# A two-block fp32 transformer kernel: where transposes, the last FFN product's token blocks and early weight loads stand

## The chip, the cores and the metric

The kernel runs on one core of a Trainium2 chip. The metric is the device time of one execution in microseconds (us), as a median of several runs. The core has five engines that run their own instruction lists and meet at semaphores: TensorE (PE, matmuls; its weight loads are listed as PEld), VectorE (DVE), ScalarE (ACT), GpSimd (POOL), and SyncE (SP), which here only issues DMAs. TensorE works with one of two clocks, 1.2 and 2.4 GHz; the profile gives the granted clock as a share of the full one.

## The reference

Two blocks, one after the other, on 1024 tokens of width 1024, all in fp32:

```python
def first_block(x, ...):
    proj = rms_norm(x, norm_mix) @ w_in
    aq, ak, av, rq, rk, rv, rg, ga, gr = jnp.split(proj, offsets, axis=-1)
    att = sliding_window_attention(aq, ak, av, att_sinks)      # 8 heads, 2 key/value heads
    ret = head_group_norm(retention_chunkwise(rq, rk, rv), ret_gn_gain) * jax.nn.silu(rg)
    merged = jax.nn.sigmoid(ga) * (att @ w_att_o) + jax.nn.sigmoid(gr) * (ret @ w_ret_o)
    x = x + merged @ w_out
    h = rms_norm(x, norm_ffn)
    x = x + (jax.nn.silu(h @ w_gate) * (h @ w_up)) @ w_down    # D_FF 2816
    return rms_norm(x, final_norm)

def second_block(x, ...):
    q, k, v, zu, zv = jnp.split(rms_norm_2(x, g_pre_mix) @ w_in, [512, 1024, 1536, 2048], axis=-1)
    sgu = spatial_gating(jax.nn.gelu(zu), jax.nn.gelu(zv), sgu_ln_g, sgu_ln_b, sgu_w, sgu_b)
    mix = jnp.concatenate([dilated_attention(q, k, v, rel_bias), sgu], axis=-1) @ w_out
    x = x + rms_norm_2(mix, g_post_mix)
    f = jnp.square(jax.nn.relu(rms_norm_2(x, g_pre_ffn) @ w_ff1)) @ w_ff2      # width 4096
    return x + rms_norm_2(f, g_post_ffn)
```

## The kernel before

**Products.** Each fp32 operand is split into a high part (type fp32r) and a low part (the rest), and a product is three matmuls: high by low, low by high, high by high. Activations stand in HH and HL (high, low), weights in WH and WL. A matmul has 128 rows of one operand and 512 columns of the other. A weight "unit" is 128x1024, loaded raw by SP into one of three slots of WRAW (`fetch`, L2505; a slot is reused once both halves of its former weights are split), rounded into WH by ACT (L1014, in FFN down products L1222) and subtracted into WL by DVE (L1476, L1762) or POOL (L2162).

**Order.** Nothing schedules the program: each engine has a Python function (`pe_program`, `act_program`, `dve_program`, `pool_program`, `sync_program`) that writes out its instructions in the order in which they run, and all of them walk the same lists of keys. `Banks` (L66) gives the eight PSUM banks to results in turn, in PE's order, so an engine may fill a bank only when what was in it before has been read.

**First projections.** After the attention projections PE runs the loop over `RVG`, groups of 24 matmuls that make the retention values: group (nh, tt) is `proj_n` (L636 to L638), 128 tokens by 512 columns. Ahead of groups 0 and 1, `values(0)` and `values(1)` (L685, matmuls of L689) transpose the tile AVT, which DVE copies out of the two banks of the projection `av` (L1546); that projection stands directly before the loop (L620 to L622). `put` moves results of both kinds from PSUM through two buffers FA, and SP stores them; `FILLS` (L347) is the list of what goes through FA, in order. From group 1 on `turn0` (L692) adds transposes of X tiles.

**FFNs.** In both blocks the up and down products follow Strassen and Winograd with seven products P1 to P7 of half-size quarters. `strassen(lay)` makes the hidden activations; they go to DRAM (`scr_h`, from the tile HS) and come back as quarters A11, A21, A12, A22 of the down product's operand (`load_quarter`, L2745, into HHF and HLF). Each quarter is loaded in two halves, here called A11/0 and A11/1. At the last block of the up product SP issues them at set steps (`FIRST_IN`): A11/0 and A21/0 when P1 has ended, A12/0 and A22/0 at P5, A11/1 and A21/1 at P2, A12/1 and A22/1 at P4. Between them it issues the first raw weights of the down product, two items in each: d0 (items 0 and 1), d1 (items 2 and 3), d2, d3 and so on. `ffn_down` (PE: L851) then runs, for each product and each chunk of the inner dimension, the items of a chunk (5 or 6 in layer 1, 8 in layer 2) by four token blocks of 128: three matmuls each (L864 to L866). An item needs its weights' two halves and its operand's two halves, DAH and DAL, which ACT and DVE make (L1219, L1759) in a ring of eight. In all products but the last PE takes an item for all four token blocks and then the next item. In the last product, P4, it takes token block by token block, all items each (L876), as the rows of a block are then complete and what follows can begin.

**Behind the down product.** DVE adds a block's product to the residual rows X (L1850, instruction L1882), after POOL has added the sum DV into X (L2351). In layer 1 the norm of the second block follows: row norms, HLF by L1935, and `back(3, tt)` (PE: L643, transposes of L650; ACT: L1027, L1031; DVE: L1484, L1489) turns the normed tokens of tile tt into HH and HL. Tiles 0 to 3 are turned between the blocks of P4, and tiles 4 to 7 in the loop over `zv` (PE L892, ACT L1332), one behind each group of 24 matmuls. Ahead of that loop PE runs the four `zu` products (L620), which need `back(3, 0)` to `back(3, 3)`. In layer 2 the last instructions are the final norm's: `fin` on DVE (L2130, L2144) with POOL's reciprocal roots (L2205) and the stores.

## Time and profile before

| what | value |
|---|---|
| median of 3 runs | 2671.52 us (2671.32 to 2673.26) |
| the profiled execution | 2674.15 us |
| its span, first to last instruction | 2672.4 us |
| mean granted TensorE clock | 0.996 |
| PE busy | 2627.6 us (98% of the span) |
| DVE, POOL, ACT busy | 1550.4, 1174.9, 1026.5 us |
| chain that ended last: PE, DVE, POOL, DMA, issue | 88%, 4%, 3%, 2%, 2% |
| largest waits of PE | L650 for DVE X 9.1 us in 2, L864 for DVE WL 5.6 us in 7, L811 for DVE HS 3.1 us, L689 for DVE AVT 2.3 us |

Times of the trace are counted from the start of the span; 1.75 us of the profiled execution lie around the span. A row of the timeline gives the start, the duration, engine, line, operation, tiles, a count, and in brackets how long the engine was idle before it and what released it. Matmuls overlap: one lasts 0.39 us, and the next starts 0.23 us after it where nothing is late, so the time lost at a wait is read from start to start.

### The profile page before, as it was taken

The numbers are of one execution on the slowest core, as the hardware profiler recorded it, in microseconds if no ns is written. First come the engines' busy times: TensorE is split into PE (matmuls) and PEld (weight loads), VectorE is DVE, ScalarE is ACT, GpSimd is POOL, SyncE is SP. The second block draws the span as 40 slices with busy tenths as digits, with TensorE's granted clock in tenths as the row PEclk, the third lists the DMA queues.
The fourth block names the chain that finished last, engine by engine and source line by source line (L and its number), as shares of the span: only waits on it lengthen the run. The fifth ranks groups of instructions, "written<-read, shape, count | busy, mean of one in ns | idle before, by whom it ended". The sixth has DMA issues, their size and how long they took to land.

```text
span 2672.4 us, 35524 instructions
## 1 busy us (share of the span) xinstructions
PE 2627.6 (98%) x13170; PEld 2203.9 (82%) x13170; DVE 1550.4 (58%) x2631; ACT 1026.5 (38%) x2053; POOL 1174.9 (44%) x933
## 2 busy tenths in 40 slices
PE   8999999999999999999999999999999999999998
PEld 7788888777888988888888778989988888878886
DVE  4325555575535544444798641167647666568787
ACT  4122333574223332322444631067634332244443
POOL 1347877344535566555232764244144544200204
PEclk9999999999999999999999999999999999999999
DMA  5555766704551222222752344233043333263524
GB/s 182 177 181 201 268 230 235 268 17 151 197 195 64 72 87 87 79 80 71 283 187 94 118 154 159 74 69 65 20 142 103 107 114 107 103 251 131 189 96 164
DMA packets 162618, 372.35 MB, mean 139 GB/s; under 512 B 21478, under 2 KB 42598, under 8 KB 158822
## 3 DMA queue, kind: packets, MB, share of 16 engines
q1 hardware_dynamic: 162446, 370.08, 40.4%
q8 instruction: 106, 1.74, 0.3%
q14 instruction: 66, 0.53, 0.1%
HBM read 267.94 MB, written 101.83 MB: 138 GB/s over the span
## 4 chain that ended last, share of the span: by engine, by line
PE 88%; DVE 4%; POOL 3%; DMA 2%; issue 2%; ACT 1%; SPq 0%; POOLq 0%; DVEq 0%; ACTq 0%
PE PS L811 12%; PE PS L813 12%; PE PS L814 12%; PE PS L864 5%; PE PS L866 5%; PE PS L865 5%; PE PS L636 4%; PE PS L638 4%; PE PS L637 4%; PE PS L965 3%; PE PS L620 3%; PE PS L621 3%; PE PS L622 3%; PE PS L749 1%; PE PS L943 1%
## 5 line engine op out<-in xcount | busy, mean ns | idle before, releaser
L2162 POOL TENSOR_TENSOR WL<-WRAW,WH 128x512 fp32r<-128x512 f32 (+1 forms) x146 | 246.7, 1690 | 363.6 <-ACT WH L1014 363.6
L811 PE MATMUL PS<-HH,WL 128*128 128x512 f32 (+1 forms) x928 | 349.3, 376 | 5.3 <-DVE HS L1804 3.1
L814 PE MATMUL PS<-HH,WH 128*128 128x512 f32 (+1 forms) x928 | 347.8, 375 | 0.0
L813 PE MATMUL PS<-HL,WH 128*128 128x512 f32 (+1 forms) x928 | 347.6, 375 | 0.0
L1476 DVE TENSOR_TENSOR WL<-TS,WH 128x512 fp32r<-128x512 f32 x216 | 227.2, 1060 | 182.0 <-ACT WH L1014 181.7
L864 PE MATMUL PS<-WH,DAL 128*128 128x512 f32 x756 | 295.8, 391 | 5.6 <-DVE WL L1762 5.6
L866 PE MATMUL PS<-WH,DAH 128*128 128x512 f32 x756 | 294.7, 390 | 0.0
L865 PE MATMUL PS<-WL,DAH 128*128 128x512 f32 x756 | 294.7, 390 | 0.0
L2351 POOL TENSOR_TENSOR X<-X,DV 128x512 f32<-128x512 f32 x56 | 90.1, 1632 | 358.2 <-DVE DV L1874 275.5
L1014 ACT ACTIVATE WH<-TS 128x512 fp32r<-128x512 f32 x216 | 130.9, 623 | 199.2 <-POOL TS L2178 199.1
L811 PEld LDWEIGHTS PS<-HH,WL 128*128 128x128 f32 x928 | 174.8, 188 | 37.2 <-DVE HS L1804 3.3
L636 PE MATMUL PS<-WH,HL 128*128 128x512 f32 x512 | 203.9, 398 | 1.2 <-DVE HL L2041 0.9
L638 PE MATMUL PS<-WH,HH 128*128 128x512 f32 x512 | 200.7, 392 | 0.0
L814 PEld LDWEIGHTS PS<-HH,WH 128*128 128x128 f32 x928 | 174.8, 188 | 31.2
L637 PE MATMUL PS<-WL,HH 128*128 128x512 f32 x512 | 200.5, 392 | 0.0
L813 PEld LDWEIGHTS PS<-HL,WH 128*128 128x128 f32 x928 | 174.8, 188 | 31.0
L1014 ACT ACTIVATE WH<-WRAW 128x512 fp32r<-128x512 f32 (+1 forms) x236 | 175.4, 756 | 61.3 <-PE PS L638 18.7
L2178 POOL TENSOR_TENSOR TS<-WRAW 128x512 f32<-128x512 f32 x108 | 143.8, 1331 | 124.4 <-issue 120.8
L1476 DVE TENSOR_TENSOR WL<-WRAW,WH 128x512 fp32r<-128x512 f32 (+1 forms) x90 | 115.1, 1280 | 105.1 <-ACT WH L1014 105.0
L864 PEld LDWEIGHTS PS<-WH,DAL 128*128 128x128 f32 x756 | 142.3, 188 | 37.7 <-issue 6.0
L1762 DVE TENSOR_TENSOR WL<-WRAW,WH 128x512 fp32r<-128x512 f32 x189 | 155.8, 824 | 24.1 <-ACT WH L1222 23.9
L866 PEld LDWEIGHTS PS<-WH,DAH 128*128 128x128 f32 x756 | 142.3, 188 | 29.9
(372 smaller groups left out, 6142.1 us busy)
## 6 DMA issues: line engine op xcount, KB each, us to landing
WRAW<-in_u_f SPq DMA_DIRECT2D x56, 512.0 KB, 3.6
WRAW<-in_u_in SPq DMA_DIRECT2D x54, 512.0 KB, 4.5
WRAW<-scr_t SPq DMA_DIRECT2D x52, 512.0 KB, 3.7
scr_h<-HS SPq DMA_DIRECT2D x96, 256.0 KB, 2.2
WRAW<-in_u_gu SPq DMA_DIRECT2D x44, 512.0 KB, 3.4
scr_t<-TTa SPq DMA_DIRECT2D x19, 1024.0 KB, 4.1
WRAW<-in_u_out SPq DMA_DIRECT2D x24, 512.0 KB, 3.5
scr_x<-X SPq DMA_DIRECT2D x24, 512.0 KB, 5.0
```

What stands on the lines that cost most here:

```text
L636: e.matmul(PS[:, b, :], HL[:, k, ts], whole_slot(WH, n)[:, cs], start=(k == 0), stop=False)
L637: e.matmul(PS[:, b, :], HH[:, k, ts], whole_slot(WL, n)[:, cs], start=False, stop=False)
L638: mm = e.matmul(PS[:, b, :], HH[:, k, ts], whole_slot(WH, n)[:, cs], start=False, stop=(k == 7))
L811: e.matmul(PS[:, b, 0:wd], wl[:, blk(kk)], op_moving(q, kk, c0, wd, 0), start=(kk == 0), stop=False)
L813: e.matmul(PS[:, b, 0:wd], wh[:, blk(kk)], op_moving(q, kk, c0, wd, 1), start=False, stop=False)
L814: mm = e.matmul(PS[:, b, 0:wd], wh[:, blk(kk)], op_moving(q, kk, c0, wd, 0), start=False, stop=(kk == 3))
L864: e.matmul(dst, hl, wh, start=(i == 0), stop=False)
L865: e.matmul(dst, hh, wl, start=False, stop=False)
L866: mm = e.matmul(dst, hh, wh, start=False, stop=(i == g - 1))
L1014: e.activation(dst, src, ACT.Copy).then_inc(*c.inc("w_hi", i))
L1476: e.tensor_tensor(lo, raw, hi.bitcast(F32), ALU.subtract).then_inc(*c.inc("w_lo_v", i))
L2162: e.tensor_tensor(lo, raw, hi.bitcast(F32), ALU.subtract).then_inc(*c.inc("w_lo_p", i))
```

## The change

In the loop over `RVG`, group 0 now stands before `values(0)` and group 1 before `values(1)`, on PE, ACT and SP, and `FILLS` has the same order. In the last product of both down products, PE takes token blocks 0 and 1 together, item by item, and then blocks 2 and 3 alone; in layer 1 `back(3, 0)` and `back(3, 1)` stand behind the pair, `back(3, 2)` and `back(3, 3)` behind block 2, and none behind block 3. DVE follows with its own order. `back(3, 4 + tt)` moves one zv group later on PE and ACT. On SP, the raw weights d0 to d2 are fetched at P6 of the last block of the up product, and the rest of the first product's (d3, in layer 2 alone) at P2, each ahead of the quarter loads of that step. Before, d0 and d1 were fetched at P7, d2 at P2 behind its quarter loads, and d3 at P4 behind its quarter loads.

```diff
--- before.py
+++ after.py
@@ -344,8 +344,8 @@
     PAIRS_OF = {1: 0, 2: FF1 // 2}
     T_SLOT = {"T3": 0, "T4": 1, "T1": 2, "T2": 3}
     RVG = [("rv", nh, tt) for nh in range(2) for tt in range(NT)]
-    FILLS = ([("aq", j, half) for half in range(2) for j in range(4)] + [("ak", 0), ("ak", 1), ("avt", 0), RVG[0],
-             ("avt", 1)] + RVG[1:])
+    FILLS = ([("aq", j, half) for half in range(2) for j in range(4)] + [("ak", 0), ("ak", 1), RVG[0], ("avt", 0), RVG[1],
+             ("avt", 1)] + RVG[2:])
     EARLY = [("ak", 0), ("ak", 1), ("av", 0)]
     IN_ORDER = [(p, 0, m, 0) for m in range(NB0) for p in ("P1", "P6", "P7", "P5", "P2", "P4", "P3")]
     LATE = [("zu", j, 1) for j in range(4)] + [("q2", j, half) for j in range(8) for half in range(2)]
@@ -697,9 +697,9 @@
             mm.then_inc(*bk.fill(("nb", 1, q, j)))
 
         for i, (_, nh, tt) in enumerate(RVG):
+            proj_n(("rv", nh, tt), [U["u_rv", 4 * nh + x] for x in range(4)], tt, tt == 0)
             if i < 2:
                 values(i)
-            proj_n(("rv", nh, tt), [U["u_rv", 4 * nh + x] for x in range(4)], tt, tt == 0)
             if 1 <= i <= len(TURN0):
                 turn0(*TURN0[i - 1])
         for j in range(4):
@@ -874,11 +874,13 @@
                         for b in range(4):
                             part(i, b)
                 else:
-                    for b in range(4):
+                    for bs in ((0, 1), (2,), (3,)):
                         for i in range(g):
-                            part(i, b)
-                        if lay == 1:
-                            back(3, b)
+                            for b in bs:
+                                part(i, b)
+                        if lay == 1 and bs[0] < 3:
+                            back(3, bs[0])
+                            back(3, bs[0] + 1)
                 for i in range(g):
                     used(DOP[lay, n, i], d_key(lay, n, 3))
             LAST[ops[DOP[lay, last - 1, g - 1]][2] + 1] = d_key(lay, last - 1, 3)
@@ -892,8 +894,8 @@
         for tt in range(NT):
             normed(3, [tt])
             proj_n(("zv", tt), [U["u_zv", i] for i in range(4)], tt, tt == 0)
-            if tt < 4:
-                back(3, 4 + tt)
+            if 1 <= tt < 5:
+                back(3, 3 + tt)
             for i in buckets_after(tt):
                 b = open_bank(("bp", i))
                 w.wait_ge(*c.at("buckets", "all"))
@@ -1078,9 +1080,9 @@
         for half in range(2):
             feed(("av", half))
         for i, key in enumerate(RVG):
+            put(key)
             if i < 2:
                 put(("avt", i))
-            put(key)
             if 1 <= i <= len(TURN0):
                 turn0(*TURN0[i - 1])
             if i < 15:
@@ -1334,8 +1336,9 @@
             w.wait_ge(*bk.full(key))
             e.activation(V2[:, tt, :], PS[:, bk.at(key), :], ACT.Gelu_apprx_tanh).then_inc(*bk.free(key))
             feed(key)
+            if 1 <= tt < 5:
+                back(3, 3 + tt)
             if tt < 4:
-                back(3, 4 + tt)
                 scale_x2(4 + tt)
         for j in range(4):
             zu(j, 1)
@@ -1907,9 +1910,10 @@
             for b in range(4):
                 add(last - 2, b)
             for b in range(4):
-                if lay == 1:
-                    back(3, b)
                 add(last - 1, b)
+                if lay == 1 and b in (1, 2):
+                    back(3, 2 * b - 2)
+                    back(3, 2 * b - 1)
                 if lay == 2:
                     fin(1, b)
             feed(d_key(lay, last - 2, 3))
@@ -2590,9 +2594,9 @@
             feed(("av", half))
             down_tiles(("av", half))
         for i, key in enumerate(RVG):
+            put(key)
             if i < 2:
                 put(("avt", i))
-            put(key)
             if i < 15:
                 feed(key)
             down_tiles(key)
@@ -2762,15 +2766,13 @@
                 for x, (p, q) in enumerate(PROD):
                     key = p, lay, m, c0
                     if (m, c0, wd) == BLOCKS[lay][-1]:
+                        while p == "P6" and n_fetch[0] <= DUNIT[lay, 0, 4]:
+                            fetch()
+                        while p == "P2" and n_fetch[0] < DUNIT[lay, 1, 0]:
+                            fetch()
                         for kind, half in FIRST_IN.get(p, ()):
                             w.wait_ge(*bk.full(key))
                             load_quarter(lay, 0, kind, half)
-                        while p == "P7" and n_fetch[0] <= DUNIT[lay, 0, 2]:
-                            fetch()
-                        while p == "P2" and n_fetch[0] <= DUNIT[lay, 0, 4]:
-                            fetch()
-                        while p == "P4" and n_fetch[0] < DUNIT[lay, 1, 0]:
-                            fetch()
                     if (lay == 2 or m % 2 == 1) and p in DONE:
                         qq = DONE[p]
                         if lay == 1:
```

SP, last block of the up product of layer 2. HHF and HLF are the quarters' tiles, `WRAW<-in_u_f` raw weights (d0 to d3 in turn), `scr_h<-HS` a store of hidden activations; in brackets are the semaphores waited for. Before:

```order
L2530 DMA WRAW<-in_u_f 128x2x512 [waits w_lo_v]
L2530 DMA WRAW<-in_u_f 128x2x512 [waits w_t,w_lo_p]
L2757 DMA HHF<-scr_h 128x4x512 [waits bank_full7]
L2757 DMA HLF<-scr_h 128x4x512
L2781 DMA scr_h<-HS 128x512 [waits f_m2]
L2757 DMA HHF<-scr_h 128x4x512 [waits h11_0,h22_0,h12_0,h21_0,bank_full0]
L2757 DMA HLF<-scr_h 128x4x512
L2530 DMA WRAW<-in_u_f 128x2x512 [waits w_lo_v]
L2781 DMA scr_h<-HS 128x512 [waits f_s]
L2757 DMA HHF<-scr_h 128x4x512 [waits bank_full1]
L2757 DMA HLF<-scr_h 128x4x512
L2530 DMA WRAW<-in_u_f 128x2x512 [waits w_lo_v]
```

and after the change:

```order
L2534 DMA WRAW<-in_u_f 128x2x512 [waits w_lo_v]
L2534 DMA WRAW<-in_u_f 128x2x512 [waits w_t,w_lo_p]
L2534 DMA WRAW<-in_u_f 128x2x512 [waits w_lo_v]
L2761 DMA HHF<-scr_h 128x4x512 [waits bank_full7]
L2761 DMA HLF<-scr_h 128x4x512
L2783 DMA scr_h<-HS 128x512 [waits f_m2]
L2534 DMA WRAW<-in_u_f 128x2x512 [waits w_lo_v]
L2761 DMA HHF<-scr_h 128x4x512 [waits h11_0,h22_0,h12_0,h21_0,bank_full0]
L2761 DMA HLF<-scr_h 128x4x512
L2783 DMA scr_h<-HS 128x512 [waits f_s]
L2761 DMA HHF<-scr_h 128x4x512 [waits bank_full1]
L2761 DMA HLF<-scr_h 128x4x512
```

d2, the third load of WRAW, moved from behind A11/1 and A21/1 (waits on h11_0 and bank_full0) up to d0 and d1, and d3, the fourth, from the last place to just ahead of A11/1. It waits for a low half made by DVE, and the quarters now stand behind that wait. In layer 1 the same holds for d2; d3 belongs there to the second product and keeps its place.

DVE, the end of the down product of layer 1: L1882 adds a block of P4 to X, L1489 makes HL for half a token tile in `back`. Before:

```order
L1878 TENSOR_TENSOR DV<-PS,DV 128x512 [waits bank_free5,bank_full5]
L1489 TENSOR_TENSOR HL<-PS,HH 128x4x128 [waits h_hi] x2
L1882 TENSOR_TENSOR X<-PS,X 128x512 [waits d_v,bank_full6]
L1489 TENSOR_TENSOR HL<-PS,HH 128x4x128 [waits h_hi] x2
L1882 TENSOR_TENSOR X<-PS,X 128x512 [waits d_v,bank_full1]
L1489 TENSOR_TENSOR HL<-PS,HH 128x4x128 [waits h_hi] x2
L1882 TENSOR_TENSOR X<-PS,X 128x512 [waits d_v,bank_full4]
L1489 TENSOR_TENSOR HL<-PS,HH 128x4x128 [waits h_hi] x2
L1882 TENSOR_TENSOR X<-PS,X 128x512 [waits d_v,bank_full7]
L1476 TENSOR_TENSOR WL<-WRAW,WH 128x1024 [waits w_hi] x3
```

and after, where the same lines are numbered 1885, 1492 and 1479:

```order
L1881 TENSOR_TENSOR DV<-PS,DV 128x512 [waits bank_free5,bank_full5]
L1885 TENSOR_TENSOR X<-PS,X 128x512 [waits d_v,bank_full6]
L1885 TENSOR_TENSOR X<-PS,X 128x512 [waits d_v,bank_full7]
L1492 TENSOR_TENSOR HL<-PS,HH 128x4x128 [waits h_hi] x4
L1885 TENSOR_TENSOR X<-PS,X 128x512 [waits d_v,bank_full4]
L1492 TENSOR_TENSOR HL<-PS,HH 128x4x128 [waits h_hi] x4
L1885 TENSOR_TENSOR X<-PS,X 128x512 [waits d_v,bank_full1]
L1479 TENSOR_TENSOR WL<-WRAW,WH 128x1024 [waits w_hi] x3
```

The add of block 1 moved ahead of all of `back(3, 0)` and `back(3, 1)`, and the last add stands behind `back(3, 3)` as the last of the group. POOL's instructions have the same order before and after.

## Rows read from the trace of the kernel before

**Rows 1.** Page, part 1: busy time, share of the span and instructions of each engine.

```profile
PE 2627.6 (98%) x13170; PEld 2203.9 (82%) x13170; DVE 1550.4 (58%) x2631; ACT 1026.5 (38%) x2053; POOL 1174.9 (44%) x933
```

**Rows 2.** Timeline, PE, values: start us, us, line, operation, count, [idle before <-releaser].

```profile
89.52 0.39 PE L622 MATMUL PS<-HH,WH 128*128 128x512 f32 x1
...
92.24 0.87 PE L689 MATMUL PS<-ID,AVT 128*128 128x128 f32 x4 [2.34 <-DVE AVT L1546]
...
99.80 0.60 PE L689 MATMUL PS<-ID,AVT 128*128 128x128 f32 x4
...
105.73 0.49 PE L696 MATMUL PS<-ID,X 128*128 128x128 f32 x3
```

**Rows 3.** Timeline, DVE: low half of the first u_rv unit, copies into AVT.

```profile
66.40 1.23 DVE L1476 TENSOR_TENSOR WL<-WRAW,WH 128x1024 fp32r<-128x1024 f32 x1 [4.50 <-ACT WH L1014]
...
91.41 1.28 DVE L1546 COPY AVT<-PS 128x512 f32<-128x512 f32 x2
```

**Rows 4.** Windows: us, busy (x) of PE, PEld, DVE, ACT, POOL, granted clock, DMA share, GB/s.

```profile
92.00:96.00 4.00, 3.76 (x12) 3.11 (x13) 0.69 (x2) 0.60 (x1) 1.71 (x1) 0.57 0.32 58
...
2345.00:2355.00 10.00, 10.00 (x46) 8.29 (x45) 7.01 (x12) 4.42 (x8) 0.00 (x0) 1.00 1.04 390
...
2376.00:2379.00 3.00, 2.78 (x7) 2.24 (x8) 3.00 (x6) 3.00 (x7) 0.00 (x0) 0.50 0.29 107
```

**Rows 5.** Timeline, PE, start of the second down product of layer 1.

```profile
1299.20 0.47 PE L864 MATMUL PS<-WH,DAL 128*128 128x512 f32 x1 [0.16 <-DVE WL L1762]
...
1305.43 0.47 PE L864 MATMUL PS<-WH,DAL 128*128 128x512 f32 x1 [0.51 <-DVE WL L1762]
```

**Rows 6.** Chain of waits, pieces in order of time, start of the down product, layer 1.

```profile
1279.39 8.76 DMA WRAW<-in_u_dn
```

**Rows 7.** Timeline, PE, layer 2: items 6 and 8 of the down product.

```profile
2367.88 0.47 PE L864 MATMUL PS<-WH,DAL 128*128 128x512 f32 x1 [0.57 <-DVE WL L1762]
...
2376.22 0.77 PE L864 MATMUL PS<-WH,DAL 128*128 128x512 f32 x1 [2.62 <-DVE WL L1762]
```

**Rows 8.** Chain of waits, same place: start us, us, piece.

```profile
2353.18 13.11 DMA WRAW<-in_u_f
...
2370.73 3.96 DMA WRAW<-in_u_f
```

**Rows 9.** Timeline, DVE, same place.

```profile
2346.67 0.68 DVE L1762 TENSOR_TENSOR WL<-WRAW,WH 128x512 fp32r<-128x512 f32 x1
...
2368.86 0.68 DVE L1826 TENSOR_TENSOR HS<-PS,HS 128x512 f32<-128x512 f32 x1
```

**Rows 10.** Operations on tile HHF, 2345 to 2348: durations ns, starts, issue to landing.

```profile
L2757 SPq DMA_DIRECT2D HHF<-scr_h x1: 359/359/359, 2345.9 to 2345.9; - x1
...
DMA to landing us min/median/max: 8.0/8.0/8.0
```

**Rows 11.** Timeline, PE, end of FFN 1 and zv loop.

```profile
1500.59 0.47 PE L620 MATMUL PS<-HH,WL 128*128 128x512 f32 x1 [1.80 <-DVE HL L1489]
...
1529.15 1.09 PE L650 MATMUL PS<-ID,HLF 128*128 128x128 f32 x8 [1.08 <-DVE HLF L1935]
```

**Rows 12.** Timeline, DVE, end of FFN 1.

```profile
1495.54 0.69 DVE L1882 TENSOR_TENSOR X<-PS,X 128x512 f32<-128x512 f32 x1 [0.59 <-POOL X L2351]
...
1501.10 4.95 DVE L1476 TENSOR_TENSOR WL<-WRAW,WH 128x1024 fp32r<-128x1024 f32 x2
```

**Rows 13.** Timeline, POOL, end of FFN 1.

```profile
1491.67 9.96 POOL L2351 TENSOR_TENSOR X<-X,DV 128x512 f32<-128x512 f32 x8
```

**Rows 14.** Timeline, PE, last product of FFN 2.

```profile
2644.47 0.47 PE L864 MATMUL PS<-WH,DAL 128*128 128x512 f32 x1 [1.26 <-DVE WL L1762]
...
2645.67 0.47 PE L864 MATMUL PS<-WH,DAL 128*128 128x512 f32 x1 [0.28 <-DVE WL L1762]
```

**Rows 15.** Timeline, POOL and DVE, last product of FFN 2.

```profile
2646.20 12.01 POOL L2351 TENSOR_TENSOR X<-X,DV 128x512 f32<-128x512 f32 x8 [5.08 <-DVE DV L1878]
...
2662.99 0.69 DVE L1882 TENSOR_TENSOR X<-PS,X 128x512 f32<-128x512 f32 x1 [1.59 <-PE PS L866]
```

## The prediction

> **What bounds the kernel now.** The page's busy times come first: PE is busy for 2627.6 us, 98% of the span [rows 1], so PE is the bound, and what a change of order can give lies in the 45 us in which PE waits. These I read next, one wait of PE at a time: in the timeline the bracket names the releaser, and the loss is the distance from start to start less the 0.23 us of a matmul that nothing holds up. Then comes the granted clock: where it is 0.5 the matmuls go at 1.2 GHz instead of 2.4, and a wait costs more than itself. Last, behind each wait, the engine that it names, to find what that engine waited for.
>
> The change touches five places where PE waits.
>
> **A, values.** The last matmul of the projection starts at 89.52, the transposes of AVT at 92.24 [rows 2]: they wait for DVE's copies, which run from 91.41 to 92.7 [rows 3]. The loss is 2.72 - 0.23 = 2.49 us. Behind it four transposes and 24 matmuls take 7.56 us (92.24 to 99.80), while the next such group takes 5.93 (99.80 to 105.73) [rows 2]; in between the granted clock is 0.57 [rows 4], so 1.63 us are lost to the lower clock. Now 24 matmuls that need no copy stand first. Their weights' first unit was split at 66.40 [rows 3], some 23 us ahead; their banks are bank 0 and on, which other results left long before. So group rv0 runs from 89.75 to 95.3, and AVT has been there since 92.7. Both losses go: **-4.1 us**. The bank that DVE's copy frees is now asked for by the transposes, 3 us after it is free. ACT's `put` of rv0 now stands ahead of the AVT results: nobody waits for those within 10 us.
>
> **B1, raw weights of FFN 1.** PE waits at 1299.20 and 1305.43 for WL, 0.16 and 0.51 us [rows 5]; each gap adds some 0.16 us until matmuls overlap again, so 0.32 + 0.67. Why: d2 was issued at 1279.39 behind quarter loads and took 8.76 us to land [rows 6]; DVE's splits of its items stand ahead of the P3 add, that add ahead of POOL's product, the store and the fetch of d3 on SP. Fetched at P6, d2 is in by about 1278. Then the chain is ended by A11/1, which now has d2's 0.5 MB ahead of it (1.3 us at the 390 GB/s that such a stretch moves [rows 4]): it lands near 1285.5, the P3 add comes 2.6 us sooner, and so do d3 and d4. 2.6 is more than 0.51: **-1.0 us**.
>
> **B2, raw weights of FFN 2.** Item 6 starts at 2367.88 [0.57] and item 8, the first of the second product, at 2376.22 [2.62] [rows 7]. d3 was issued at 2353.18 and took 13.11 us, since three quarter halves were ahead of it on a queue at 390 GB/s; it landed at 2366.3 [rows 4, 8]. DVE splits items 4 to 7 before the P3 add (2368.86 [rows 9]); the store of that block follows, and only then d4, issued at 2370.73, 3.96 us [rows 8], landing at 2374.7. Back from item 6 without its wait (2367.15), at 12 matmuls or 2.73 us an item, item 4 is due at 2361.7 and item 8 at 2372.6. The losses are 0.73 at item 6, 2.62 + 0.16 at item 8 and, from 2376 to 2379 at clock 0.50 [rows 4], half of some 3.2 us, 1.6. After: d2 goes out with d0 and d1 and lands near 2346.3. d3 waits for the low half of item 1, which DVE starts at 2346.67 [rows 9], is issued near 2347.5 and lands near 2354. A11/1, which had landed at 2345.9 + 8.0 = 2353.9 [rows 10], has 1 MB more ahead of it, 2.7 us at 390 GB/s: near 2356.6, 5 us before item 4 is due. The P3 add is then paced by A11/1 and four splits of some 1.2 us, near 2362. d4 follows 1.9 us later as before (2368.86 to 2370.73), lands near 2368, and ACT and DVE need the 1.5 us that they need now (2374.7 to 2376.22): 2369.5 against 2372.6. All three losses go: **-5.1 us**.
>
> A rule of the Trainium skill bears on this, in DMA: Bandwidth & Descriptors, section "Queues, rings and completion order": descriptors of a ring are taken in the order in which they were queued. By it an early d3 has to push A11/1 back by its full size, and that is the 2.7 us worked out above from the 390 GB/s. The trace agrees, as the late d3 took 13.11 us behind the quarters [rows 8].
>
> **C1, end of FFN 1.** The first zu matmul starts at 1500.59 [1.80] [rows 11]. It waits for HL of `back(3, 3)`, which is behind the adds on DVE. These go at the pace of POOL, whose eight adds of 1.25 us run from 1491.67 to 1501.6 [rows 13]; block 1's add starts at 1495.54 [rows 12]. Moving the transposes earlier doesn't change POOL. After: adds 0 and 1 on DVE (until 1496.15), `back(3, 0)` and `back(3, 1)`, four HL of 0.6, add 2, four more HL: 1496.15 + 2.4 + 0.6 + 2.4 = 1501.6, where before the last HL was done just ahead of 1500.59. (L1882 and L1489 handle tiles of one shape, 0.6 us apart.) The banks say the same of PE: `back(3, 3)` takes the bank that the add of block 1 frees at 1496.15, so PE stands for about 2 us before block 3 instead of 1.8 us before zu, and zu starts at 1501.9. That is **+1.3 us**: the wait moves and grows. **C1b**: in the zv loop PE waits at 1529.15 for HLF [1.08] [rows 11], 1.24 us with the gap; one group (5.5 us) later HLF is there. **-1.2 us**. The next `back` has a small wait of the same kind, taken as nothing.
>
> What comes behind C1: DVE's two splits of units start at 1501.10 and take 4.95 us together [rows 12], where one alone takes 1.23 [rows 3]; POOL works beside them. They now start a little later. The Trainium skill, SBUF — State Buffer, section "SBUF: two separate sides", says that a DVE operation with two inputs in SBUF and a GpSimd operation lock each other out for the whole instruction, so that the one that comes second waits for the other. By it the first split would go from behind POOL's split instead of ahead of it, and be ready up to 3 us later; the 4.95 us agree. By my rows, the second zu product starts 5.4 us after the first, near 1507.3, and splits that end at 1506 to 1507.5 just make it. I take 0 and keep 1 us for the range.
>
> **C2, end of FFN 2.** PE waits at 2644.47 [1.26] and 2645.67 [0.28] [rows 14]: the last product's block 0 needs an item each 0.68 us, and DVE, between other work, makes the low half of the last item just ahead of 2645.67. With two blocks per item it needs one each 1.36 us; the 1.26 + 0.28 and two gaps, 1.86 us, go, and PE ends 1.9 us sooner. Behind PE stand DVE's add of the last block at 2662.99 and 9.4 us of norm and store up to the end. POOL's adds into X take until 2658.2 [rows 15] and don't move, but the last block's add comes only at 2661. Between 1.4 and 1.9, as the norm of block 2 comes closer to POOL's: **-1.4 us**.
>
> **The sum**: -4.1 - 1.0 - 5.1 + 1.3 - 1.2 - 1.4 = -11.5 us. The profiled execution took 2674.15 us and would take 2662.6; the median of the runs is 2.6 below it, and the same sum against 2671.52 gives 2660.0. That is my forecast.
>
> **The rivals.**
> - *The wait just moves, and the clock goes with it.* The new 2 us of PE before block 3 at 1494 could be followed by a stretch at half clock, as after the 2.34 us of A and the 2.62 us of B2; that of 1.80 at 1500.59 was not. Price 1.6, and 1 us more if the second zu product comes late: 2661.6 to 2662.6. For it: 2.0 lies between 1.80 and 2.34.
> - *B gives little.* If the early raw weights only push the quarters back, and the P3 add stays where it is, B2's 5.1 stays: 2665.1. Against it: item 4 has 5 us to spare.
> - *C2 gives nothing.* If blocks 0 and 1, handed over together, make DVE and POOL the last ones at the end: 2661.4. For it: POOL is busy until 2658.2 [rows 15].
> - *The change doesn't do what it says at A*: rv0 waits for weights or a bank. Then 4.1 less: 2664.1. Against it: 66.40 [rows 3].
> - *Slower than before.* On SP, d3's fetch waits for a low half with A11/1, A21/1, A12/1 and A22/1 queued behind it. If DVE reaches that half later than at 2346.67 by more than 5 us, item 4 waits, and with it everything. A delay of w then costs w - 5 at item 4, and B2's 5.1 isn't gained, which leaves 6.4 of the gain: even at w = 11.4, and slower by 0.2% (5.3 us) from w = 16.7, at 2676.9. Nothing on DVE holds that half back so long: what is ahead of it are splits of 0.68.
>
> **How the numbers follow.** Forecast, all terms within their bounds, 2657.5 to 2662.5: 0.57. The moved wait with the clock: 0.14. B gives little, or half: 0.09. C2 nothing: 0.05. A nothing: 0.04. Two of these together, or something that I don't see, near no change: 0.07. Slower: 0.04. A measurement of this kernel can tell about 0.2%, 5.3 us, from no change, so faster means below 2666.2. The first five cases lie below it, the sixth within 0.2% (B and A nothing: 2669.2). Faster 0.57 + 0.14 + 0.09 + 0.05 + 0.04 = 0.89, same 0.07, slower 0.04. The range reaches from 2656, where the bounds of C1 (0 instead of +1.3), C2 (-1.9) and small waits (-0.9) add up, to 2665.5, which takes in B giving little.
>
> **What would show it.** In the profile after: no wait before L689 near 95 and clock 1.00 from 92 to 96; turn0's first transposes near 101.6; no wait above 0.3 us at items 6 and 8 of FFN 2 and no stretch at 0.5 near 2364 to 2370; d3 landing before 2356; a wait of PE of about 2 us inside P4 of layer 1, and nearly none before zu; HLF's wait in the zv loop gone; PE's last matmul about 12 us earlier. Wrong it would be with A11/1 landing after item 4 is due, or with a half-clock stretch at a place that had none.

## The result and the profile after

Over 20 runs of each kernel in turns, the changed kernel took 2671.03 us in the median (2658.05 to 2676.21) and the kernel before 2675.39 (2671.10 to 2689.16); the ratio on record is 0.9961, with a 95% interval of 0.9944 to 0.9978, so 10.4 us faster (6 to 15). The ratio of the two medians alone would be 0.9984, 4.4 us. These numbers can't be read without knowing that the executions of both kernels fall into two groups, a short one at a mean granted clock of 0.995 to 0.998 and a long one at 0.990 to 0.993, and that the medians depend on how many fell into which. Over all runs of this study the kernel before has 60 short executions (median 2672.4) and 57 long ones (2686.4), with one of 3300 us at a clock of 0.749 left out; the changed kernel has 9 short (2659.4) and 11 long (2674.0). Group against group it is 13.1 and 12.4 us faster. My forecast was 11.5, given as 2660.0 against a median of before that came from short executions alone; the profiled execution of after is a short one too, 2659.72 us, with a span of 2657.9 instead of 2672.4. What the long group is, is told behind the experiments.

Page of the changed kernel, busy times and the chain that ended last:

```profile
PE 2622.1 (99%) x13170; PEld 2202.3 (83%) x13170; DVE 1550.7 (58%) x2631; ACT 1027.2 (39%) x2053; POOL 1177.2 (44%) x933
...
PE 90%; DVE 4%; POOL 3%; issue 1%; DMA 1%; ACT 1%; POOLq 0%; DVEq 0%; SPq 0%; ACTq 0%
```

PE has 5.5 us less of busy time for the same matmuls, some 3.2 of them from the two stretches at half clock that are gone (A and B2), and 9 us less of waiting.

**Values.** Timeline of PE, the places of [rows 2], and windows of the granted clock (the second one covers the start of the second product of layer 2, for below):

```profile
89.62 0.39 PE L636 MATMUL PS<-WH,HL 128*128 128x512 f32 x1
...
95.07 0.60 PE L689 MATMUL PS<-ID,AVT 128*128 128x128 f32 x4
...
101.00 0.60 PE L689 MATMUL PS<-ID,AVT 128*128 128x128 f32 x4
...
101.44 0.60 PE L696 MATMUL PS<-ID,X 128*128 128x128 f32 x4
```

```profile
92.00:96.00 4.00, 4.00 (x22) 3.31 (x21) 0.06 (x1) 0.67 (x2) 1.36 (x1) 1.00 0.34 124
...
2366.00:2372.00 6.00, 6.00 (x28) 4.99 (x27) 6.00 (x11) 5.59 (x12) 0.00 (x0) 1.00 0.34 122
```

Group rv0 starts at 89.62, the transposes of AVT stand behind it and wait for nothing, and turn0 begins at 101.44 instead of 105.73. From the last matmul of the projection to there it is 12.04 us instead of 16.21.

**Start of the FFN 2 down product.** SP's queue and DVE's P3 add, for [rows 8 to 10]:

```profile
2339.90 0.37 SPq L2534 DMA_DIRECT2D WRAW<-in_u_f  x1
...
2340.83 0.36 SPq L2761 DMA_DIRECT2D HHF<-scr_h  x1
...
2355.58 8.17 SPq L2534 DMA_DIRECT2D WRAW<-in_u_f  x4
```

```profile
2353.71 0.68 DVE L1829 TENSOR_TENSOR HS<-PS,HS 128x512 f32<-128x512 f32 x1
```

d3 (2339.90) took 5.6 us to land instead of 13.11; A11/1 (2340.83) took 7.3. The product itself starts 7.54 us earlier than before, so on the scale of before d3 landed at 2353.0, A11/1 at 2355.7, the P3 add came at 2361.3 and d4 was issued at 2363.1. PE had no wait at items 6 and 8, and the clock stayed at 1.00. From the first matmul of L864 to the 61st PE took 46.04 us before and 40.80 now. In layer 1, where the whole product starts 4.20 us earlier, the P3 add came 5.47 us behind the first matmul instead of 8.15, 2.7 us sooner.

**End of FFN 1.** POOL, PE and DVE, for [rows 11 to 13]:

```profile
1482.14 2.38 POOL L2166 TENSOR_TENSOR WL<-WRAW,WH 128x1024 fp32r<-128x1024 f32 x1 [2.13 <-ACT WH L1016]
...
1484.48 10.00 POOL L2355 TENSOR_TENSOR X<-X,DV 128x512 f32<-128x512 f32 x8
```

```profile
1482.76 1.16 PE L650 MATMUL PS<-ID,HLF 128*128 128x128 f32 x8 [0.72 <-DVE DV L1881]
...
1489.19 1.16 PE L650 MATMUL PS<-ID,HLF 128*128 128x128 f32 x8 [0.76 <-DVE X L1885]
...
1494.68 0.47 PE L620 MATMUL PS<-HH,WL 128*128 128x512 f32 x1 [0.69 <-DVE HL L1492]
```

```profile
1488.36 0.69 DVE L1885 TENSOR_TENSOR X<-PS,X 128x512 f32<-128x512 f32 x1 [1.80 <-POOL X L2355]
...
1494.94 4.12 DVE L1479 TENSOR_TENSOR WL<-WRAW,WH 128x1024 fp32r<-128x1024 f32 x2
```

PE waits twice by some 0.7 us inside the product, and 0.69 us before zu, where it had one wait of 1.80 and three of 0.2 to 0.4. In the zv loop the transposes behind the second group start without a wait; before, this was the row at 1529.15:

```profile
1527.44 1.03 PE L650 MATMUL PS<-ID,HLF 128*128 128x128 f32 x8
```

**End of FFN 2.** PE's last matmul, POOL and DVE:

```profile
2647.72 0.39 PE L866 MATMUL PS<-WH,DAH 128*128 128x512 f32 x1
```

```profile
2637.19 8.27 POOL L2355 TENSOR_TENSOR X<-X,DV 128x512 f32<-128x512 f32 x5
```

```profile
2648.56 0.68 DVE L1885 TENSOR_TENSOR X<-PS,X 128x512 f32<-128x512 f32 x1
...
2653.55 1.28 DVE L2134 SCALAR_TENSOR_TENSOR X<-XG,SM,NXb 128x1024 f32<-128x1024 f32 x1 [0.44 <-POOL SM L2209]
```

The last add comes at 2648.56, the last product of the norm at 2653.55. Segment by segment, in us, from the starts of the same instructions in the two profiles:

| segment | forecast | measured |
|---|---|---|
| up to turn0 (A) | -4.1 | -4.3 |
| FFN 1, first 61 matmuls of L864 (B1) | -1.0 | -1.2 |
| from there to zu (C1) | +1.3 | -0.5 |
| zu to the second attention (C1b) | -1.2 | -1.8 |
| FFN 2, first 61 matmuls of L864 (B2) | -5.1 | -5.2 |
| from there to the end (C2) | -1.4 | -1.66 |
| all else | 0 | +0.3 |
| sum | -11.5 | -14.4 |

Five of the six terms are within 0.6 us of the forecast, and one has the wrong sign: C1.

### The profile page after: what moved, and what is told of

It is laid out like the page before. It is cut to its first block, busy times and chain, and to the rows that moved or that the text cites. A ratio compares the mean times of both kernels' runs of the same rounds, so it can differ in the third digit from the quotient of the medians.

```text
span 2657.9 us, 35523 instructions
## 1 busy us (share of the span) xinstructions
PE 2622.1 (99%) x13170; PEld 2202.3 (83%) x13170; DVE 1550.7 (58%) x2631; ACT 1027.2 (39%) x2053; POOL 1177.2 (44%) x933
## 4 chain that ended last, share of the span: by engine, by line
PE 90%; DVE 4%; POOL 3%; issue 1%; DMA 1%; ACT 1%; POOLq 0%; DVEq 0%; SPq 0%; ACTq 0%
PE PS L811 13%; PE PS L813 13%; PE PS L814 13%; PE PS L866 6%; PE PS L864 6%; PE PS L865 6%; PE PS L636 3%; PE PS L638 3%; PE PS L637 3%; PE PS L967 3%; PE PS L620 3%; PE PS L621 3%; PE PS L622 3%; PE PS L749 1%; PE PS L945 1%
## 5 line engine op out<-in xcount | busy, mean ns | idle before, releaser
L864 PE MATMUL PS<-WH,DAL 128*128 128x512 f32 x756 | 294.3, 389 | 0.0
L811 PEld LDWEIGHTS PS<-HH,WL 128*128 128x128 f32 x928 | 174.7, 188 | 37.2 <-DVE HS L1807 3.3
L865 PEld LDWEIGHTS PS<-WL,DAH 128*128 128x128 f32 x756 | 141.9, 188 | 29.6
L864 PEld LDWEIGHTS PS<-WH,DAL 128*128 128x128 f32 x756 | 141.9, 188 | 29.4 <-DVE DV L1881 0.2
```

Source lines behind the costliest of these rows:

```text
L811: e.matmul(PS[:, b, 0:wd], wl[:, blk(kk)], op_moving(q, kk, c0, wd, 0), start=(kk == 0), stop=False)
L864: e.matmul(dst, hl, wh, start=(i == 0), stop=False)
L865: e.matmul(dst, hh, wl, start=False, stop=False)
```

## The experiments

Each kernel was profiled once and timed. As the two groups blur medians of ten runs, I read each part in its segment of the profile, and the times group by group.

### Part A alone

The hunks on `FILLS` and on the three `RVG` loops, on the kernel before.

> The kernel before with part A alone: group rv0 ahead of values(0), rv1 ahead of values(1), nothing else. My theory: both the wait of PE before L689 (2.34 us) and the half-clock stretch behind it (1.63 us) go, so that turn0's first transposes start near 101.6 instead of 105.73, and all that follows is 4.1 us earlier; the waits further on are those of the kernel before. Rival (the clock falls somewhere else instead): the stretch at half clock turns up later and only 2.5 us are won.

```profile
94.04 0.60 PE L689 MATMUL PS<-ID,AVT 128*128 128x128 f32 x4
...
100.41 0.60 PE L696 MATMUL PS<-ID,X 128*128 128x128 f32 x4
```

turn0 begins at 100.41. PE reached the last matmul of the projection at 88.37, 1.15 us earlier than in the profile of before and ahead of every edit; from there it took 12.04 us, as in the changed kernel. The waits further on are in the same places, but not of the same size: in layer 2 the wait at item 6 (0.57 us before) is missing, as d3 took 11.79 us to land instead of 13.11, and the stretch to the 61st matmul took 44.91 us instead of 46.04. Seven short executions have a median of 2670.8, three long ones 2685.9, so 1.6 and 0.5 us less than before; the short ones alone spread over 7 us, so these times can't tell 2.5 from 4.1. The profiles of other kernels can: the stretch at half clock behind this wait isn't always there. In the profile of part C1 alone, which has the old order here, PE waits as before:

```profile
88.60 0.39 PE L622 MATMUL PS<-HH,WH 128*128 128x512 f32 x1
...
91.32 0.63 PE L689 MATMUL PS<-ID,AVT 128*128 128x128 f32 x4 [2.33 <-DVE AVT L1548]
...
97.26 0.60 PE L689 MATMUL PS<-ID,AVT 128*128 128x128 f32 x4
...
103.18 0.60 PE L696 MATMUL PS<-ID,X 128*128 128x128 f32 x4
```

```profile
91.00:95.00 4.00, 3.68 (x19) 3.14 (x20) 0.78 (x2) 0.60 (x1) 1.81 (x1) 1.00 0.30 56
```

The window has clock 1.00, and turn0 begins 14.58 us after the last projection matmul, against 16.21 in the profile of before. The 1.63 us of the clock are real in one execution and absent in another; of the six profiles with the old order at this place three have the stretch, the kernel before among them, and three do not. Against the 12.04 us of the new order, A is thus worth 2.5 us in three of these profiles and 4.1 to 4.2 in the other three.

### Part B alone, and one step of it

The SP hunk alone.

> The kernel before with the SP part alone: raw weights of the down products' first items fetched at P6 and P2 of the last block. My theory: 1.0 us in layer 1 (waits at 1299.20 and 1305.43 gone) and 5.1 us in layer 2 (waits of items 6 and 8 and the half-clock stretch gone), 6.1 in all. Rival: the quarters land later by as much as the weights land sooner, so item 4 of layer 2 waits and only 0 to 3 us are won.

From the first to the 61st L864 it took 40.80 us in both layers, as in the changed kernel: 1.2 and 5.2 us saved against the profile of before. Other profiles with the old order have 42.02 to 42.23 us in layer 1 and 44.91 to 45.99 in layer 2, so that B is worth 1.2 to 1.4 and 4.1 to 5.2 us. Short executions 2666.9 (3), long ones 2680.4 (7), so 5.5 and 6.0 us less. The rival is out: no item waited for its quarter.

Then one line only:

```diff
+                        while p == "P4" and n_fetch[0] < DUNIT[lay, 1, 0]:
+                            fetch()
                         for kind, half in FIRST_IN.get(p, ()):
                             w.wait_ge(*bk.full(key))
                             load_quarter(lay, 0, kind, half)
...
-                        while p == "P4" and n_fetch[0] < DUNIT[lay, 1, 0]:
-                            fetch()
```

> The kernel before with one line moved on SP: at P4 of the last block, the fetch of what is left of the first down product (d3, in layer 2) stands ahead of the loads of A12/1 and A22/1 instead of behind them; d0 to d2 stay. It asks how much of part B hangs on how early d3 is. By 1 MB at 390 GB/s d3 lands 2.7 us sooner, 2363.6 instead of 2366.3 on the scale of the kernel before; item 6's wait (0.57) goes, the P3 add and d4 come 2.7 us sooner, so the 2.62 us at item 8 become 0 to 0.3, and with them the half-clock stretch goes: 4.5 to 5.1 us in layer 2, nearly all of the SP part. Rival (the two steps that the changed kernel moves it are needed): at least 1.5 us of wait stay at item 8. Layer 1 has no d3 in this product and stays as it was.

DVE and SP in this kernel:

```profile
2362.39 0.68 DVE L1826 TENSOR_TENSOR HS<-PS,HS 128x512 f32<-128x512 f32 x1
...
2351.77 0.37 SPq L2530 DMA_DIRECT2D WRAW<-in_u_f  x1
...
2364.26 1.82 SPq L2530 DMA_DIRECT2D WRAW<-in_u_f  x3
```

d3 took 7.5 us to land, so at 2359.3. Counted from the product's first matmul it landed 6.6 us sooner than before and not 2.7: it was issued 1.0 us earlier, and the two half quarters that were ahead of it are 2 MB, not 1 as I had written. The P3 add came at 2362.39, d4 at 2364.26, and the segment took 40.80 us. The whole of the 5.2 us of layer 2 thus hangs on one place: d3 ahead of the last two quarter halves. Seven short executions: 2667.0, 5.4 less than before; three long ones: 2681.7. That d2 and d3 go even earlier in the changed kernel adds nothing in layer 2; what d2 adds is the 1.2 us of layer 1.

### Part C1 alone, and the changed kernel without it

PE's pair and DVE's order, for layer 1 only:

```diff
-                    for b in range(4):
+                    for bs in (((0, 1), (2,), (3,)) if lay == 1 else ((0,), (1,), (2,), (3,))):
```

> The kernel before with the pair of token blocks in the last product of layer 1 alone (PE, and DVE's order), back(3, 4 + tt) left in its place. Measured from the start of POOL's eight adds into X (1491.67 in the kernel before, zu at 8.92 us behind it), my theory has zu's first matmul at 10.2 us behind it, so 1.3 us later. Rival (the pair itself makes zu start sooner, as the changed kernel's zu started 0.7 us sooner than parts A and B explain): zu at 8.9 us or less behind the start of POOL's adds. If the start of POOL's adds moves, it is by the load of the first zu weights, which takes 5.53 us in the profile of before and 3.79 in that of after.

```profile
1487.58 10.02 POOL L2354 TENSOR_TENSOR X<-X,DV 128x512 f32<-128x512 f32 x8
```

```profile
1497.79 0.47 PE L620 MATMUL PS<-HH,WL 128*128 128x512 f32 x1 [0.63 <-DVE HL L1491]
```

zu came 10.21 us behind the start of POOL's adds, in the changed kernel 10.20, in kernels without the pair 8.9 (8.87 to 9.32 in seven). The +1.3 us of the forecast is right, as a distance from POOL's start. The short executions of this kernel took 2671.6 (8) and the long ones 2688.3 (2), against 2672.4 and 2686.4: no difference that these few can tell. What moved is the start of the adds. The chain of waits leads from it back through POOL's and ACT's halves of the first zu weights to their load, here in the changed kernel, then in the kernel before:

```profile
1477.19 3.79 DMA WRAW<-in_u_in
```

```profile
1482.61 5.53 DMA WRAW<-in_u_in
```

Without the pair this load took 5.53, 5.19, 5.3, 5.3, 5.5, 5.4 and once 4.5 us; with the pair 3.79, 3.53, 3.5, 3.6 and 3.4, but 4.6 and 5.4 in two more kernels. It is issued 158.0 us behind the 61st matmul in both profiles shown, so the place of the issue didn't move. SP issues two more of the same size within 0.9 us behind it; the one after those, issued alone, took 3.3 to 3.5 us in every kernel. So with the pair the first load is mostly faster by 1.7 us, but not always, and I have no row that says why. That stays open.

The other direction, PE and DVE of layer 1 as before, all else as changed:

> The changed kernel with one part undone: in the last product of layer 1 PE takes token block by token block again, with back(3, b) behind each, and DVE has its old order; back(3, 4 + tt) keeps its new place one zv group later. My theory: zu's first matmul 8.9 us behind the start of POOL's adds instead of 10.2; the load of the first zu weights, 5.2 to 5.5 us in the kernels without the pair and 3.5 to 3.8 with it so far, takes about 5.3 again, so that the two cancel and the time stays within 0.5 us; the wait of PE for HLF in the zv loop (0.7 to 1.3 us in all kernels with the old place) stays gone. Rival (the load's duration has nothing to do with the pair): 3.8 us, and 1.3 us faster than the changed kernel.

zu 8.9 us behind POOL's start, load 5.3 us, no wait in the zv loop, span 2657.4 (2657.9 with the pair), and the five short executions at 2659.9 against 2659.4 (the three long ones at 2676.3 against 2674.0). In these runs the pair in layer 1 gives nothing: in the distance from the 61st matmul to zu, the seven kernels without it have 175.3 to 176.0 us and the five with it, and POOL's split in its old place, 175.2 to 176.4. Where the load took about the same, the 1.3 us come out: 176.4 with the pair and a load of 4.64 us (the changed kernel with the wait filled, below), where PE stood for 1.60 us inside the product, and 175.3 without the pair and a load of 4.48 us (part B alone).

What does give something is the later `back` in the zv loop. With the old place PE waited there for HLF by 0.69 to 1.39 us, and in one profile by 3.65, with half clock behind it:

```profile
1529.63 1.09 PE L650 MATMUL PS<-ID,HLF 128*128 128x128 f32 x8 [3.65 <-DVE HLF L1938]
```

### Part C2 alone, and with two pairs

> The kernel before with the pair of token blocks in the last product of layer 2 alone. My theory: waits of 1.26 and 0.28 us near 2644 gone, PE's last matmul 1.9 us earlier, the end 1.4 to 1.9 us earlier. Rival: DVE and POOL become the last ones and the end moves by less than 0.5 us.

The waits near 2644 are gone, from the 61st matmul to PE's last it took 263.61 us instead of 265.69, and 10.21 us follow instead of 9.79: 1.66 us in all, the same as in the changed kernel. Short executions 2669.9 (6), 2.5 less; of the others three are long (2680.2 to 2686.7) and one lies between, 2674.6 at a clock of 0.994. The next kernel gives the last two blocks to PE as a pair too:

```diff
-                    for bs in ((0, 1), (2,), (3,)):
+                    for bs in (((0, 1), (2,), (3,)) if lay == 1 else ((0, 1), (2, 3))):
```

> The changed kernel, but in layer 2's last product blocks 2 and 3 are a pair as well. PE needs no more weights per time than it has, so its end stays. My theory: both last blocks come at PE's end, DVE and POOL have two norms behind it instead of one, and the kernel ends 2 to 3 us later. Rival (DVE and POOL are behind anyway): within 0.5 us.

DVE in this kernel, the adds of blocks 2 and 3 and the last product of the norm:

```profile
2662.47 0.69 DVE L1885 TENSOR_TENSOR X<-PS,X 128x512 f32<-128x512 f32 x1 [5.64 <-PE PS L866]
...
2665.69 0.68 DVE L1885 TENSOR_TENSOR X<-PS,X 128x512 f32<-128x512 f32 x1
...
2670.69 1.28 DVE L2134 SCALAR_TENSOR_TENSOR X<-XG,SM,NXb 128x1024 f32<-128x1024 f32 x1 [0.44 <-POOL SM L2209]
```

PE ends as in the changed kernel, but the add of block 2 waits until then (2662.47; PE's last matmul starts at 2662.73), that of block 3 stands 3.2 us behind it, and from PE's last matmul to the end it is 12.3 us instead of 10.2: 2.1 us slower. Short executions 2660.9 (4), long ones 2676.5 (6), 1.6 and 2.5 more than the changed kernel. A last block alone is worth that.

### What sets zu: a later split

If POOL's eight adds set when zu starts, then POOL's split ahead of them is what to move:

```diff
-                    feed(d_key(lay, last - 3, 3))
+                    if lay == 2:
+                        feed(d_key(lay, last - 3, 3))
                 for b in range(4):
                     add_v("21", "P7", b)
                     add_v("22", "P7", b)
+                    if lay == 1 and b == 1 and k == len(CHUNKS[lay]) - 1:
+                        feed(d_key(lay, last - 3, 3))
```

and on DVE `back(3, 2)` and `back(3, 3)` stand ahead of the add of block 2.

> The changed kernel with POOL's split of the first zu unit moved behind four of its eight adds into X at the end of layer 1, and on DVE the add of block 2 moved behind back(3, 2) and back(3, 3). Theory (POOL's adds, started late by a load, set when zu starts): the adds start some 1.9 us sooner, PE's wait for the bank of block 1's add (0.76 us) goes, and zu starts 1.3 to 1.7 us sooner, the kernel is as much faster. Rival (the load and the split themselves become the last ones): zu moves by less than 0.5 us.

POOL and PE:

```profile
1482.95 5.04 POOL L2358 TENSOR_TENSOR X<-X,DV 128x512 f32<-128x512 f32 x4 [2.68 <-DVE DV L1881]
...
1487.95 2.39 POOL L2169 TENSOR_TENSOR WL<-WRAW,WH 128x1024 fp32r<-128x1024 f32 x1
...
1490.28 5.07 POOL L2358 TENSOR_TENSOR X<-X,DV 128x512 f32<-128x512 f32 x4
```

```profile
1483.02 1.16 PE L650 MATMUL PS<-ID,HLF 128*128 128x128 f32 x8 [0.71 <-DVE DV L1881]
...
1492.83 0.39 PE L620 MATMUL PS<-HH,WL 128*128 128x512 f32 x1
...
1547.17 1.87 PE L902 MATMUL PS<-OH,RB 33*8 33x512 f32 x4 [0.88 <-DMA RB<-in_c_one]
```

From the 61st matmul to zu it took 173.41 us instead of 175.52, and PE went into zu without a wait: 2.1 us. POOL's adds started 163.5 us behind the 61st matmul instead of 165.3. Two orders changed at once here, POOL's and DVE's, and no run separates them. From zu to the second block's attention this profile then took 249.78 us instead of 246.64 and so gave the gain back: a wait of 0.41 us at the second zu product, and 55 us behind zu one of 0.88 us for the table of relative positions, whose load SP issued at 1543.11, 1.1 us later than in the changed kernel, with 3.4 us at half clock behind it. Two short executions at 2657.6, ten long at 2670.0: 1.7 and 4.0 us less than the changed kernel. The theory on POOL holds for the start of zu, and the next one in line was a load.

## The long executions

The profile of part B alone is a long one. PE and windows of it in the second block's attention:

```profile
1746.14 1.30 PE L965 MATMUL PS<-V,PT 128*128 128x64 f32 x10 [1.06 <-DVE PT L2049]
```

```profile
1740.00:1745.00 5.00, 5.00 (x26) 3.12 (x24) 3.65 (x18) 4.55 (x8) 0.68 (x2) 1.00 0.33 92
...
1748.00:1756.00 8.00, 8.00 (x30) 6.18 (x29) 2.53 (x9) 2.62 (x6) 4.01 (x4) 0.50 0.41 83
...
1764.00:1771.00 7.00, 7.00 (x31) 6.47 (x30) 2.58 (x9) 1.56 (x5) 0.00 (x0) 0.50 0.50 88
```

PE waits 1.06 us for DVE; in every kernel here that doesn't fill this wait it is 1.06 to 1.09. In the short profiles the clock stays at 1.00 behind it. In the three profiles that are long (part B alone, the later split, the two pairs) it is 0.50 for 23.9 us, beginning 0.9 to 1.5 us behind the end of the wait, where the products are small. The 200 matmuls behind the wait then take 37.2 us instead of 26.1, and from the wait to FFN 2's down product a long profile takes 12 to 14 us more than a short one in all. To see whether the wait starts it, ten 128x128 transposes of the identity were put into the wait, whose result is overwritten:

```diff
+                if q == 0:
+                    for _ in range(10):
+                        e.transpose(PS[:, b, 0:128], ID[:, :], ID[:, :])
                 w.wait_ge(*c.at("vr", 7))
                 w.wait_ge(*bk.out(("t1", q)))
```

> About half of the executions of every kernel so far, the kernel before too, are 12 to 14 us longer, at a mean clock of 0.991 instead of 0.996 to 0.998. The one such profile (part of the SP experiment) has a clock of 0.50 from 1748 to 1771 us, in the second block's attention, from 2 us behind a wait of PE of 1.06 us. This kernel is the changed one with ten extra 128x128 transposes of the identity in that wait, whose result is overwritten. Theory (the wait lets the clock fall): hardly any of the executions is in the long group, so that the median falls from about 2671 to 2659. Rival (the small matmuls of that stretch do it, wait or not): still 4 to 6 in 10. Slower by up to 0.3 us if the transposes outlast the wait.

> The kernel before with the ten identity transposes in the 1.06 us wait of the second block's attention and nothing else. Theory (that wait lets the clock fall for some 23 us in about half of the executions): none or hardly one of the executions in the long group of 2682 to 2690, median near 2672. Rival (the fill has no part in it, and the six short executions of the filled changed kernel were luck): 4 to 6 in 10 in the long group, median 2672 to 2684.

PE in the filled changed kernel:

```profile
1741.98 1.31 PE L964 MATMUL PS<-ID 128*128 128x128 f32 x10
...
1743.13 1.23 PE L970 MATMUL PS<-V,PT 128*128 128x64 f32 x10
```

The products behind it start when they did, 246.66 us behind zu for 246.64. None of 6 executions was long on the changed kernel (2659.8 to 2665.8, median 2662.2), and none of 12 on the kernel before (2670.9 to 2676.0, median 2673.4, the longest at a clock of 0.994), while 11 of the 23 executions of the kernel before beside it were long. The rival with luck is out. The times are not those of the short group throughout, though: 2662.2 is 2.8 us above the short executions of the changed kernel. The one filled execution that was profiled has nothing of it at the fill, as from the filled wait to FFN 2's down product it took 601.7 us for 602.0; where the other five lost it isn't shown. Is it the wait, though, or the added work? The same ten transposes directly behind the wait:

> The changed kernel with the same ten identity transposes as the filled kernel, but behind the wait of the second block's attention instead of in it: PE does the same extra work and still stands for 1.06 us first. Theory (the standing itself starts the long stretch at half clock): 4 to 6 executions in 10 are in the long group of 2671 to 2677 again, though not one of the 24 of the three filled kernels was; the short ones 1.2 us longer than the changed kernel's. Rival (extra matmuls of 128 rows near that place keep the clock up, the wait has no part): none or hardly one in the long group.

```profile
1740.77 1.28 PE L967 MATMUL PS<-ID 128*128 128x128 f32 x10 [1.06 <-DVE PT L2056]
```

Two of 12 were long (2675.3 and 2677.7), ten short with a median of 2661.8. That lies between the two theories and decides for neither. Two of 12 against 0 of 24 comes by chance about one time in ten, and three kernels without any fill had only 2 or 3 long ones in 10 (parts A and C1 alone, and d3 one step earlier). What is shown is that ten transposes in the wait keep the long group away: 0 of 24 in three kernels, against 57 of 117 of the kernel before. Whether they do it by ending the wait or as added work isn't shown.

All of it together, with the seven small products of the table spread over the last three zv groups, so that they don't meet their load:

> The changed kernel with what the runs pointed to: POOL's split of the first zu unit behind four adds, DVE's add of block 2 behind back(3, 3), the ten identity transposes in the 1.06 us wait of the second block's attention, and the seven small products of the relative-position table spread over the last three zv groups instead of four (2, 3, 2), since the first of them waited 0.88 us for its load in the run with the later split. Expected: no execution or hardly one in the long group; zu 1.3 to 2 us sooner than in the changed kernel; no wait before the table's products; median 2656 to 2659. Rival (the zu gain is given back somewhere again): median 2659 to 2661, as the filled kernel alone.

```profile
1491.05 0.39 PE L620 MATMUL PS<-HH,WL 128*128 128x512 f32 x1
```

zu starts at 1491.05 without a wait, the table's products have none, the span is 2653.7, and the six executions took 2655.5 to 2661.0, median 2659.2, all short: a ratio of 0.9920 (0.9893 to 0.9947) to the kernel before, 21 us, against 0.9961 of the changed kernel. It has the lowest median of all. But that median misses the forecast of 2656 to 2659 and falls where the rival had it, 2659 to 2661, and it equals that of the changed kernel's short executions (2659.4). By these numbers most of what the 21 us are above the changed kernel's 10 is the missing long group; the earlier zu shows in the profile, and in the medians, of six executions each, as 2.9 us against the filled kernel.

## Why the prediction was right, and where it was not

- **A** was right in size (-4.3, of which 0.1 came ahead of the edit), but 1.63 of it hangs on a stretch at half clock that three of six profiles with the old order do not have. I took one execution's clock for the kernel's.
- **B1 and B2** were right step by step: A11/1 at 2355.7 (forecast 2356.6), d3 at 2353.0 (2354), the P3 add at 2361.3 (2362), d4 issued at 2363.1 (2363.9), no wait at items 6 and 8. A11/1 came only 1.8 us later than before instead of 2.7: SP issued it 2.5 us later, behind d3 and the wait that goes with d3, and it then took 7.3 us instead of 8.0. In layer 1 the P3 add came 2.7 us sooner (2.6). What I didn't see is that a single step of d3 would have done layer 2, and that the 5.1 us belong to a d3 that took 13.11 us: in the profile of part A, where it took 11.79, the loss was 4.1.
- **C1** had the wrong sign, -0.5 for +1.3. The step that failed is that POOL's adds start where they did. The 1.3 us behind them were measured, 10.20 us for 8.92. But their start hangs on a load that took 3.79 us instead of 5.53, and I had fixed it at the row of one execution. The wait of about 2 us that I expected inside the product was 0.76 with this load, and 1.60 in the filled kernel, whose load took 4.64. Why the load was faster stays open.
- **C1b** was -1.8 for -1.2: I had taken the small second wait as nothing, and it cost 0.4 us with its gaps. The first wait also varies between executions (0.69 to 3.65 us).
- **C2** was 1.66, inside 1.4 to 1.9: PE ended 2.1 us sooner, and what follows took 0.4 us more.
- **Behind C1**: DVE's two splits started at 1494.94, now behind POOL's at 1494.43, and took 4.12 us together, while POOL's took 2.40 instead of 3.38. The rule of the Trainium skill (SBUF — State Buffer, "SBUF: two separate sides") that the first one holds the port for its whole instruction agrees with that. The second zu product, due 5.4 us behind the first at 1494.68, had its split at 1499.1 and didn't wait.
- **Rivals**: none came to pass. The new waits of 0.7 us were followed by clock 1.00. The wait of 2 us whose stretch at half clock the first rival priced did not arise; the longest one at that place, 1.60 us in the filled kernel, was followed by clock 1.00, so for 2 us the rival is untested.
- **What I left out** is larger than any term: the long group of executions, 14 to 15 us. My three runs of before were all short ones, so the range of 2656.0 to 2665.5 speaks of short executions; 11 of 20 of the changed kernel were longer than it. The difference between the kernels is nearly the same in both groups, so the direction and size held.
- **The total** came nearer than its parts. The ratio on record gives 10.4 us for my 11.5, but the two profiles differ by 14.4 and the groups by 13.1 and 12.4. That 10.4 lies so close is in part luck, as the ratio depends on how many executions of each kernel were long. The lower end of my range was also added up wrongly: the bounds that I named give 2657.3, not 2656.

## What to carry to other kernels

Ask of each wait what its chain hangs on at the far end; when that is a load, its duration in one profile is a draw, not a constant, and the term needs its spread. A stream of loads ahead of a phase is paced by where the smallest urgent one stands: moving 0.5 MB ahead of 2 MB gave 4.1 to 5.2 us. And where PE had waited for one microsecond ahead of small products, half of the executions were 14 us longer, so look at the granted clock of more than one execution before costing anything.

## What the runs showed of the hardware

- A wait of PE of 2.33 or 2.34 us was followed by 3.4 us at half clock in three profiles and by none in three others, at the same place in the same order of instructions.
- A wait of 1.06 us ahead of small products was followed by 23.9 us at half clock in the three profiles of long executions and by none in the short ones; 57 of 117 executions of the kernel before were long, and none where ten identity transposes filled the wait (0 of 24).
- A load of 0.5 MB issued on an idle queue, with two more right behind it, took between 3.4 and 5.5 us to land at the same place of the program; the next one, issued alone, took 3.3 to 3.5 us.
